# A token-tile cross-attention, another order in the pooling and gating mixer, and more PSUM banks at the end of the feed-forward part

## The reference, cut to what matters

```
x = layer_norm(alpha*x + mix(x))            # layer 0: mixer_ab, layer 1: mixer_c
x = layer_norm(alpha*x + cross_attend(x, mem))
x = layer_norm(alpha*x + conv_ffn(x))

mixer_ab:     uv = gelu(x @ w_in[:, :1024]);  u, v = halves of 512
              v = layer_norm(v);  y_a = u * (block-masked token mixing of v + b_s)
              xb = x @ w_in[:, 1024:1536]; pooled = trailing mean(windows 2,4,8,16) - xb
              y = concat(y_a, (pooled @ pool_w) * pool_scale) @ w_out
cross_attend: q = x @ wq; 4 heads of width 256, 256 memory tokens
              y = softmax(q k^T / 16) v @ wo
conv_ffn:     a, g = halves of x @ w_up (2 x 2816)
              y = (gelu(causal 3-tap conv(g) + b) * a) @ w_down
```

## Time and profile before

| what | value |
|---|---|
| time, three runs | 2064.20, 2070.85, 2075.99 us (median 2070.85) |
| the profiled execution's own time | 2074.79 us |
| its span, first to last instruction | 2072.9 us |
| mean granted TensorE clock | 0.981 |
| PE, busy share of the span | 95% |
| share of PE in the chain that ended last | 91% |

### The profile page before, as it was taken

One profiled execution on the slowest core, in us unless ns is written; L12 is line 12 of the kernel. 1 busy time (PEld: TensorE's weight loads), 2 busy tenths in 40 slices (PEclk: granted clock), 3 DMA queues, 4 the chain that ended last, 5 costly groups with the idle time before them and its releaser, 6 DMA issues.

```text
span 2072.9 us, 26714 instructions
## 1 busy us (share of the span) xinstructions
PE 1966.1 (95%) x10582; PEld 1614.9 (78%) x10582; DVE 757.5 (37%) x1747; ACT 246.2 (12%) x575; POOL 181.7 (9%) x186
## 2 busy tenths in 40 slices
PE   6998999899999999899999998799999999899997
PEld 3597576589999999899999955677776977487774
DVE  3300132207985876676522014231112213231112
ACT  1021232002442111000000010100000001010000
POOL 0100000000142321122222000000000000000000
PEclk9999999999999999999999999999999999799999
DMA  5453343334698887678888682234443434054431
GB/s 195 143 182 133 135 148 122 142 110 165 243 355 324 310 309 256 241 281 294 290 312 324 223 354 102 82 122 163 163 142 123 162 122 163 0 183 146 158 142 61
DMA packets 62724, 395.10 MB, mean 191 GB/s; under 512 B 6944, under 2 KB 6944, under 8 KB 24112
## 3 DMA queue, kind: packets, MB, share of 16 engines
q1 hardware_dynamic: 42048, 306.20, 41.2%
q0 software_dynamic: 20032, 85.50, 11.1%
q10 hardware_dynamic: 560, 2.21, 0.3%
HBM read 388.61 MB, written 5.24 MB: 190 GB/s over the span
## 4 chain that ended last, share of the span: by engine, by line
PE 91%; DVE 3%; issue 3%; DMA 2%; ACT 1%; POOL 0%; ACTq 0%; DVEq 0%; POOLq 0%
PE ps L378 24%; PE ps L710 16%; PE ps L718 13%; PE ps L429 8%; PE ps L453 7%; PE ps L387 5%; PE ps L908 5%; PE ps L623 3%; PE ps L651 1%; PE ps L401 1%; DMA arena<-v_rows,sparse_pairs 1%; PE ps L731 1%; PE ps L875 1%; PE ps L855 1%; DMA small<-small_params 1%
## 5 line engine op out<-in xcount | busy, mean ns | idle before, releaser
L378 PE MATMUL ps<-xT,ring 128*128 128x256 f32 x2048 | 450.7, 381 | 10.6 <-DVE arena L1733 9.3
L378 PEld LDWEIGHTS ps<-xT,ring 128*128 128x128 f32 x2048 | 390.3, 191 | 71.6 <-issue 17.6
L718 PE MATMUL ps<-arena,ring 128*128 (+1 forms) x2048 | 340.9, 328 | 0.0
L710 PE MATMUL ps<-xT,ring 128*128 128x192 f32 x2048 | 339.2, 327 | 0.8 <-DVE sel L1519 0.8
L718 PEld LDWEIGHTS ps<-arena,ring 128*128 128x128 f32 x2048 | 334.4, 191 | 0.5 <-issue 0.5
L710 PEld LDWEIGHTS ps<-xT,ring 128*128 128x128 f32 x2048 | 332.2, 190 | 1.0 <-DVE sel L1519 1.0
L429 PE MATMUL ps<-ring,arena 128*128 128x512 f32 x384 | 167.1, 593 | 4.4 <-DVE arena L1763 2.8
L453 PEld LDWEIGHTS ps<-xT,ring 128*128 128x128 f32 x1280 | 144.1, 192 | 2.4 <-issue 2.4
L429 PEld LDWEIGHTS ps<-ring,arena 128*128 128x128 f32 x384 | 72.3, 190 | 92.9 <-issue 86.4
L453 PE MATMUL ps<-xT,ring 128*128 128x128 f32 x1280 | 144.6, 275 | 0.0
L1723 DVE TENSOR_SCALAR arena<-arena,small 128x256 f32<-128x256 f32 x44 | 15.5, 353 | 314.4 <-ACT arena L1160 314.4
(11 more groups left out here) (236 smaller groups left out, 1444.3 us busy)
## 6 DMA issues: line engine op xcount, KB each, us to landing
ring<-stream SPq DMA_DIRECT2D x292, 1024.0 KB
arena<-second_params POOLq DMA_DIRECT2D x1, 6144.0 KB, 33.2
kv_scratch<-arena POOLq DMA_DIRECT2D x4, 1024.0 KB, 9.2
arena<-kv_scratch POOLq DMA_DIRECT2D x1, 4096.0 KB, 16.9
arena<-second_params POOLq DMA_DIRECT2D x1, 1536.0 KB, 6.7
xres<-x_in_dram ACTq DMA_DIRECT2D x1, 1024.0 KB, 10.6
arena<-mem_T POOLq DMA_DIRECT2D x1, 1024.0 KB, 5.2
arena<-u_rows,sparse_pairs POOLq DMA_INDIRECT x64
```

The costliest lines, as they stand in the source:

```text
L378: ins = pe.matmul(ps[:, bank, t * T:(t + 1) * T], w[:, k * 2 * P + t * P:k * 2 * P + (t + 1) * P], act[:, k, :], start=(k == 0), stop=(k = ...
L710: ins = pe.matmul(ps[:, o % 2, 0:DENSE], w[:, (o % 2) * D + k * P:(o % 2) * D + (k + 1) * P], xT[:, k, 0:DENSE], start=(k == 0), stop=(k = ...
L718: ins = pe.matmul(ps[:, 4 + k // 2, c:c + DENSE], w[:, (o % 2) * D + k * P:(o % 2) * D + (k + 1) * P], H[:, n, :], start=False, stop=last, ...
```

## The change

Mixer AB: the slots come in the order pool (2), v (2), u (2). TensorE makes xb, then v, then turns xT, then makes u. VectorE does the trailing means first, then v's layer norm.

Cross-attention: by token tile. `tiles_in` signals each query slot of tile 0 (`q_psum`), ScalarE copies it, and the scores of tile 0 for all four heads (banks 6 and 7) stand between the two tiles of the query projection. After the query projection come the turns of tile 0's probabilities, the scores of tile 1, tile 0's values, and then `tiles_out`, in which the turns of tile 1 stand before tile 0's last slot and the values of tile 1 before tile 1's first. Softmax steps are on pairs of heads. The copies are shared by ScalarE and VectorE. The values use a moving operand of 128 columns (one tile) and not 256.

Feed-forward: blocks 16 to 21 use banks j % 4.

Loads: the 1.5 MB load is issued among the row fetches of the expert stage (after the 45th of 64); 1 MB of normalisation parameters and 2 MB of keys and values follow at `arena_free`, and further pieces (1 MB each; the second 2 MB of keys and values) after later normalisations, each when the piece before has landed.

```diff
+def up_bank(j):
+    return j if j < 4 else j % 2 if j < 2 * FT_PAIRS + 2 else j % 4
...
-            ("ab_uv", 4), ("ab_pool", 2), ("ab_out", 4),
+            ("ab_pool", 2), ("ab_vu", 4), ("ab_out", 4),
...
@@ TensorE, tiles_in
+                        elif between:
+                            ins.then_inc(q_psum, 1)
+                    if i == 0 and between:
+                        between()
@@ TensorE, mixer AB
             pe.wait_ge(x2_ready, 4)
+            for s in range(2):
+                w = slot("ab_pool", s)
+                feature_major(w, s, xT).then_inc(slot_done, 1)
+            def ab_half(c):
...
+            ab_half(0)
+            pe.wait_ge(xb_copied, 2)
             for i in range(TT):
...
                     ins.then_inc(xt_psum, 1)
+            ab_half(1)
             pe.wait_ge(xres_back, 4)
-            for s in range(2):
-                w = slot("ab_pool", s)
-                feature_major(w, s, xT).then_inc(slot_done, 1)
@@ TensorE, cross
+                def xscores(i):
+                    for h in range(XH):
+                        pe.wait_ge(xq_ready, 8 * layer + 4 * i + h + 1)
                         for k in range(2):
+                            ins = pe.matmul(ps[:, 6 + h // 2, (h % 2) * T:(h % 2 + 1) * T],
+                                            xqT[:, 2 * h + k, i * P:(i + 1) * P],
+                                            xkT[:, 2 * h + k, :], start=(k == 0), stop=(k == 1))
...
+                def xturn(i):
+                    for b in range(2):
+                        pe.wait_ge(xprob_ready, 4 * layer + 2 * i + b + 1)
+                        for n in range(4):
+                            ins = pe.transpose(ps[:, (4, 2)[i] + b, n * P:(n + 1) * P],
+                                               xprob[:, 2 * b + n // 2, (n % 2) * P:(n % 2 + 1) * P], ident)
+                        ins.then_inc(xPT_psum, 1)
+                def xvalues(i):
+                    for b in range(2):
+                        pe.wait_ge((xPT_ready, xPT_by_dve)[b], 2 * layer + i + 1)
+                        for n in range(4):
+                            h, d = 2 * b + n // 2, n % 2
+                            for k in range(2):
+                                ins = pe.matmul(ps[:, b, n * P:(n + 1) * P],
+                                                xv[:, k, (2 * h + d) * P:(2 * h + d + 1) * P],
+                                                xPT[:, h, k, :], start=(k == 0), stop=(k == 1))
+                        ins.then_inc(xo_psum, 1)
+                def first_scores():
+                    pe.wait_ge(kv_in, 16 * (layer + 1))
+                    xscores(0)
+                tiles_in(3 + 3 * layer, lambda s: slot(f"q{layer}", s), range(4), between=first_scores)
+                xturn(0)
+                xscores(1)
+                xvalues(0)
+                def step_out(i, s):
+                    if i == 0 and s == 3:
+                        xturn(1)
+                    if i == 1 and s == 0:
+                        xvalues(1)
+                    if s == 0:
+                        pe.wait_ge(xo_ready, 2 * layer + i + 1)
+                    if s == 2:
+                        pe.wait_ge(xo_by_dve, 2 * layer + i + 1)
+                tiles_out(lambda s: slot(f"o{layer}", s), y2_tile, 4 + 3 * layer, ready=step_out)
@@ TensorE, feed_forward
-                for j in range(2 * FT_PAIRS + 2, FT):
-                    up(j, j % 2, d0 + j - 1)
                 first_tail = 2 * FT_PAIRS
+                for j in range(first_tail + 2, FT):
+                    prior = j - 2 if j < first_tail + 4 else j - 16 if j < first_tail + 6 else j - 4
+                    up(j, up_bank(j), d0 + prior + 1)
@@ ScalarE, cross (its order)
+                turned(n, 0)
+                for s in range(3):
+                    query_copy(0, s)
+                turned(n, 1)
+                query_copy(0, 3)
+                xexp(0, 0)
+                xexp(0, 1)
                 for s in range(4):
+                    query_copy(1, s)
+                xturned(0)
+                xexp(1, 0)
+                xexp(1, 1)
+                xout(0)
+                xturned(1)
+                xout(1)
@@ VectorE, cross (its order)
+                for i in range(TT):
+                    for b in range(2):
+                        xmax(i, b)
+                    for b in range(2):
+                        xscale(i, b)
+                    if i == 1:
+                        xout(0)
+                    xturned(i)
+                xout(1)
                 layer_norm(3 * layer + 1, START[f"o{layer}"] + 4)
@@ GpSimd
                     fetch(v_rows, m, m % 4)
+                    if m == 44:
+                        pool.dma_start(second[:, 0:N_SECOND_EARLY], second_d[:, 0:N_SECOND_EARLY])\
+                            .then_inc(second_early_in, 16)
...
+            load_ln(0)
+            load_kv(0)
...
             for k in range(7):
                 ln_inverse(k)
+                if 1 <= k <= 5:
+                    load_ln(k)
+                if k == 2:
+                    load_kv(1)
```

More of the change, by code:

```diff
@@ L438, in y2_tile, with tiles_in @@
                 return y2T[:, k, i * P:(i + 1) * P]
-            def tiles_in(n, weights, banks):
+            def tiles_in(n, weights, banks, between=None):
                 held = []
@@ L840, in _ @@
             pe.wait_ge(y2_by_act, 4)
-            tiles_out(lambda s: slot("ab_out", s), y2_tile, 3, ready=lambda i: pe.wait_ge(y2_by_dve, i + 1))
+            tiles_out(lambda s: slot("ab_out", s), y2_tile, 3,
+                      ready=lambda i, s: pe.wait_ge(y2_by_dve, i + 1))
             def cross(layer):
-                n0 = 8 * layer
                 xkT, xv = xkT_of[layer], xv_of[layer]
[L846 to L873, removed]
-                        for k in range(2):
[L875 to L888, removed]
@@ L1095, in _, with turned @@
                 act.activation(dots[:, 1, :], dots[:, 0, :], ACT.Gelu_apprx_tanh).then_inc(dot_gelu, 1)
[L1097 to L1101, removed]
-            act.wait_ge(arena_free, 1)
[L1104 to L1111, removed]
+            def turned(n, i):
+                act.wait_ge(xt_psum, 4 * n + 2 * i + 1)
+                act.copy(xT[:, 0:4, i * P:(i + 1) * P],
+                         ps[:, turn_banks(n, i)[0], :].rearrange("p (k t) -> p k t", k=4)).then_inc(xT_by_act, 1)
+            act.wait_ge(arena_free, 1)
             for q in range(2):
@@ L1115, in _, with ab_half @@
                          ps[:, q, :].rearrange("p (g t) -> p g t", g=2)).then_inc(xb_copied, 1)
+            def ab_half(c):
+                act.wait_ge(slot_done, START["ab_vu"] + 2 * c + 2)
+                for i in range(TT):
+                    ins = act.activation((v_sb, u_sb)[c][:, i, :], ps[:, 4 + 2 * c + i, :], ACT.Gelu_apprx_tanh)
+                ins.then_inc(act_step, 1)
+            ab_half(0)
+            for q in range(4):
+                act.wait_ge(xt_psum, 8 + q + 1)
+                act.copy(xres[:, q // 2, (q % 2) * 512:(q % 2 + 1) * 512], ps[:, q, :]).then_inc(xres_back, 1)
+            ab_half(1)
             for q in range(2):
@@ L1123, in cross @@
             def cross(layer):
-                n0 = 8 * layer
-                for s in range(4):
[L1126 to L1149, removed]
+                n = 3 + 3 * layer
@@ new lines, in xturned, with xout @@
+                def xturned(i):
+                    act.wait_ge(xPT_psum, 4 * layer + 2 * i + 1)
+                    act.copy(xPT[:, 0:2].rearrange("p h k t -> p (h k t)"), ps[:, (4, 2)[i], :]).then_inc(xPT_ready, 1)
+                def xout(i):
+                    act.wait_ge(xo_psum, 4 * layer + 2 * i + 1)
+                    act.copy(y2T[:, 0:4, i * P:(i + 1) * P], ps[:, 0, :].rearrange("p (k t) -> p k t", k=4))\
+                        .then_inc(xo_ready, 1)
+                turned(n, 0)
@@ L1176, in _ @@
             act.wait_ge(y2_by_dve, 2)
-            turned(3)
             cross(0)
-            turned(4)
+            for i in range(TT):
+                turned(4, i)
             act.wait_ge(pads_zero, 2)
             feed_forward(0)
-            turned(5)
+            for i in range(TT):
+                turned(5, i)
             for j in range(KT):
@@ L1190, in _ @@
             act.wait_ge(c_ready, KT)
-            turned(6)
             cross(1)
-            turned(7)
+            for i in range(TT):
+                turned(7, i)
             act.wait_ge(pads_zero, 3)
@@ L1606, in _ @@
             dve.wait_ge(pads_zero, 1)
[L1608 to L1618, removed]
-                dve.tensor_tensor(v, v, sgu_ln[:, 1, :], ALU.add).then_inc(uv_ready, 1)
             dve.wait_ge(xb_copied, 2)
@@ new lines, in xout @@
+                def xout(i):
+                    dve.wait_ge(xo_psum, 4 * layer + 2 * i + 2)
+                    dve.tensor_copy(y2T[:, 4:8, i * P:(i + 1) * P], ps[:, 1, :].rearrange("p (k t) -> p k t", k=4))\
```

(4 more changed lines are left out.)

108 lines of the change are left out of this document (66 added, 42 removed).

## The result

| kernel | median us (runs) | ratio to before, 95% interval |
|---|---|---|
| before | 2072.5 (4) | |
| changed | 2014.3 (4, from 2009.3 to 2018.5) | 0.9726 [0.9701, 0.9751] |
| changed, a second study of 6 runs | 2012.9 (2009.6 to 2014.7) | 0.9706 [0.9677, 0.9736] |

The change makes the kernel 2.7 to 2.9% faster, 58 us by the medians of the first study. Forecast were 2009 us and a gain of 61.9; the range of 1999 to 2026 holds the time. The second study, taken later, has eleven runs of the kernel before with a median of 2072.9 beside it.

The account below looks back on a forecast made before the run. TensorE, busy 95%, bounds the kernel through its work, waits and low clock. Gains 9.4 + 39.0 + 13.5 = 61.9 took 2074.8 to 2012.9, then 3.9 off for the median: 2009 us, range 1999 to 2026.

Parts of the forecast that it names:

- Mixer AB, 60.4 to 51.0: Mixer AB, first product to output product: means and copy to `xres` hidden under v and u; gain 9.4 us (8.4 to 12.6).
- the exposed tail: Mixer AB, before the output product: last part of VectorE's gating and copy not hidden, 0.5 us (0 to 1.5).
- Cross-attention, 15.8 us a layer at full clock: Both attentions: only TensorE's own work remains, no waits; gains 14.3 us in layer 0, 24.7 in layer 1, 39.0 together.
- The closest cover: Attention: ScalarE's copy, queued behind tile 1's last exponential, fits under scores and values; 0 us, up to 1 a layer if missed.
- The layer norm's slack: Attention output: VectorE's layer norm of tile 0, behind its copy of tile 1's values, finishes 2.4 us before TensorE asks.
- Feed-forward tail, 13.5: Last six up blocks, both layers: four banks remove waits and low clock, 41.4 us each; gain 13.5 us (9.3 if low clock reappears).
- Loads, 0: Early 1.5 MB load in the expert stage and later parameter pieces: no effect, 0 us, at most 6.7 for the early load.
- The 3.9 us taken off at the end: Whole kernel: profiled execution was 3.9 us above the three-run median 2070.85, so forecast 2012.9 became 2009.
- low clock in the attention: Rival: attention work stays at half speed, 15.8 us for each layer that has it, 2025 or 2041 us; chance 0.09.
- moved waits: Rival: attention covers fall short, a third of the 20.0 us of waits returns, 8 to 15 us, 2020; chance 0.10.
- starved stream: Rival: weight ring slot late in the expert stage, 6.7 us, or output slots uncovered by the shorter attention, 2016; chance 0.05.
- The fourth, slower than before: Rival: query projection, attention and output product of both layers all at low clock, 83 us more than before, 2154; chance 0.02.

Follow-up runs that it names:

- e2: Kernel before with the token-tile cross-attention alone (old loads, old mixer order, old feed-forward tail): 2033.1 us, ratio 0.9818 [0.9791, 0.9846].
- b1_again: Kernel before, unchanged, profiled once more for the length of its two attentions: 2063.4 us, attentions 30.2 and 32.7 us.
- e4_old_loads: Changed kernel with the old loads (1.5 MB, 4 MB and 6 MB, all after the expert stage): 2012.3 us, ratio 0.9720 [0.9690, 0.9750].

## Why the prediction was right, point by point

- *Mixer AB, 60.4 to 51.0*: 51.05. The low clock at the start stayed, 17.06 us against 13.8; the exposed tail was 0.4 us where 0.5 was taken. Right in the changed kernel, and worth less by itself, in front of the old attention.
- *Cross-attention, 15.8 us a layer at full clock*: 15.8 in both. The closest cover was named rightly: ScalarE's copy of tile 0's first two heads ended at 1315.52, 1.1 us before the values did. The layer norm's slack was taken as 2.4 us: it ended at 1342.65, TensorE asked at 1345.11, 2.5 us on (timeline of the changed kernel):

```profile
1314.94 0.58 ACT L1174 COPY arena<-ps 128x512 f32<-128x512 f32 x1
```

```profile
1335.45 1.28 DVE L1701 SCALAR_TENSOR_TENSOR xres<-xres,ps 128x512 f32<-128x512 f32 x2
...
1341.43 1.22 DVE L1715 TENSOR_TENSOR xres<-xres,arena 128x1024 f32<-128x1024 f32 x1
```

- *The pace that the Trainium skill gives for weight loads and matmuls* (TensorE: Matmul & The Clock Gate, "Back-to-back issue gap"): the 32 value records took 3.57 us, 0.112 each, where by that estimate, a factor of 1.45, it would have been 0.162; the factor is not seen. The page's 81 ns itself is shorter than a record here, so these float32 records don't test it.
- *Feed-forward tail, 13.5*: 41.44 in both layers, 6.8 and 6.7 less in the profile; 12.2 us [8.3, 16.0] by itself in time.
- *Loads, 0*: 0.
- *The base of the sum.* Profile against profile the three terms came out to the tenth, 61.9. The span fell by 57.8, as the first block ended 1.3 us later, within its scatter, and mixer C's product met 3.0 us of low clock. In time it was 58. The mis-sized term is the attention of before: 30.2 + 40.5 = 70.6 us is one execution's pair; the other three profiles of the same attention behind the old mixer have 62.9, 65.3 and 70.6. Their mean is 67.4, so the gain there is 36 on the average and not 39; e2's 37.7 allows either. The bounds left room downward for the new kernel's clock only; the length of what is removed had a spread too.
- *The 3.9 us taken off at the end* are in part the same thing counted twice. The profiled execution of before was above the median; b1_again was 11.4 us faster than it, and 7.7 of these lie in the two attentions. The gain was counted from the slow execution, and its excess was then taken off as well. The 2012.9 before that step is 1.4 us from the measured median, the 2009 behind it 5.3; with runs that spread over 9 us this is an argument and not shown by the distance alone.
- The parts add in ratio: 0.59 + 1.82 + 0.28 = 2.69% for the three alone, 2.74% together. Each of the three has an interval of 0.2 to 0.3% either way, so an interplay of some us, as mixer and old attention have it, could hide in this.
- *Rivals.* No low clock in the attention, no moved waits, no starved stream. The fourth, slower than before, had the right cause in the wrong kernel: it was the old attention that could lose up to 10.3 us a layer to the low clock.

## What to carry to other kernels

When an engine at 95% has short waits in a chain of small steps, count the chain's pure work at the pace of its undisturbed stretches and look for independent work of the same engine, here the other token tile, to put between the steps; here, in the attentions and at the feed-forward tail, all that lay over the pure work came back. Check every cover in the order of the queue of the engine that must deliver, its other copies included. And price what is removed from more than one execution when the clock takes part in it: one profile's 40 us was another's 33.

## What the runs showed of the hardware that I had not expected

The same instructions with the same waits took from 30.2 to 40.5 us for an attention. The granted clock over the whole of it was 1.00 at 30.2 us, 0.90 at 32.7, 0.73 at 37.9, 0.70 at 39.4 and 0.66 at 40.5. PE stood idle for 12.3 us of it in the shortest and in the longest alike and was busy for 17.8 and 28.2, so all of the difference is the level of TensorE's clock. And taking waits out of one stretch can go with more low clock in another: with the new mixer order the attention 58 us further on took 8 us more on the average, in three profiles of three more than in any of the four with the old order. Nor does a wait of 2.8 us cost the same each time: ahead of mixer C's output product the 56 records behind it took 24.3 us in most profiles (granted clock 1.00), 26.0 in e4_old_loads (0.93) and 27.3 in the changed kernel's first (0.89).
